# Where the weights, the normed input and the arena begin in a partition: 0 and 32 bytes past a multiple of 64, in a 1-core fp32 kernel of five network layers

## What is computed

```python
for i in range(DEPTH):                       # 4 layers
    h = _rmsnorm(x, norm_mix_g[i])
    mix = ...                                # h @ w_in, the mixer itself, @ w_out
    x = x + mix
    x = x + _sqrelu_mlp(_rmsnorm(x, norm_mlp_g[i]), mlp_w1[i], mlp_w2[i])

def _sqrelu_mlp(h, w1, w2):
    return jnp.square(jax.nn.relu(h @ w1)) @ w2
```

## The kernel before

| Tensors | Role in line 432 | Before | mod 64 | After | mod 64 |
|---|---|---|---|---|---|
| raw / wh / wl | weights (stationary) | 16544 / 32928 / 49312 | 32 | 16512 / 32896 / 49280 | 0 |
| x / xh / xl | moving (xh, xl) | 65696 / 82080 / 98464 | 32 | the same | 32 |
| rs, acc, tmp, hf, ones and other small ones | - | 114848 and on | 32 | the same | 32 |
| arena: hh, hl, yh, yl, mh, ml, the mixers' tensors | moving | 131200 and on | 0 | 131232 and on | 32 |

## Time and profile before

### The profile page before, as it was taken

The page is one execution under the profiler, slowest core; times in us unless marked ns, Lnnn a source line. Parts: engine busy times, 40 slices in busy tenths (PEclk is TensorE's granted clock), DMA queues, the critical chain, the costliest instruction groups (busy, mean ns, idle before and its releaser), DMA issues.

```text
span 4019.4 us, 50973 instructions
## 1 busy us (share of the span) xinstructions
PE 3751.5 (93%) x20972; PEld 3021.8 (75%) x20972; DVE 1907.7 (47%) x2121; ACT 1127.8 (28%) x1283; POOL 438.5 (11%) x425
## 2 busy tenths in 40 slices
PE   7999999899999999998999997867899988989998
PEld 5678888688888888866788785645699956768886
DVE  7654333353445534366534345566343356455342
ACT  2632223131222322235322222233211122333221
POOL 1111111020110201110101110000001000102011
PEclk9999999699999999999999997988999989999999
DMA  3132323032322333221333220211300013323221
GB/s 126 55 96 94 94 94 100 32 94 94 94 94 95 95 102 95 96 86 55 108 99 94 84 84 0 89 55 58 110 2 3 3 36 136 103 80 100 94 94 63
DMA packets 295680, 320.51 MB, mean 80 GB/s; under 512 B 5811, under 2 KB 287798, under 8 KB 295255
## 3 DMA queue, kind: packets, MB, share of 16 engines
q1 hardware_dynamic: 288439, 295.92, 23.3%
q0 software_dynamic: 3616, 15.86, 1.2%
q10 hardware_dynamic: 3456, 6.29, 0.4%
HBM read 307.57 MB, written 10.49 MB: 79 GB/s over the span
## 4 chain that ended last, share of the span: by engine, by line
PE 87%; DVE 7%; ACT 4%; issue 1%; DMA 0%; SPq 0%; POOL 0%; ACTq 0%; DVEq 0%; POOLq 0%
PE ps L432 70%; PE ps L773 2%; PE ps L1392 1%; PE ps L419 1%; PE ps L1411 1%; DVE wl L386 1%; PE ps L1364 1%; PE ps L1410 1%; PE ps L1371 1%; PE ps L1053 1%; ACT wh L382 1%; PE ps L1032 1%; PE ps L891 1%; PE ps L892 1%; DVE rs L456 0%
## 5 line engine op out<-in xcount | busy, mean ns | idle before, releaser
L432 PE MATMUL ps<-xh,wh 128*128 128x512 f32 x2424 | 970.1, 400 | 66.8 <-DVE wl L386 52.0
L432 PE MATMUL ps<-xl,wh 128*128 128x512 f32 x2424 | 956.4, 395 | 0.0
L432 PE MATMUL ps<-xh,wl 128*128 128x512 f32 x2424 | 954.4, 394 | 0.0
L386 DVE TENSOR_TENSOR wl<-raw,wh 128x2048 fp32r<-128x2048 f32 x283 | 657.0, 2322 | 457.9 <-ACT wh L382 457.2
L382 ACT ACTIVATE wh<-raw 128x2048 fp32r<-128x2048 f32 x283 | 539.6, 1909 | 883.2 <-PE ps L432 756.2
L432 PEld LDWEIGHTS ps<-xh,wh 128*128 128x128 f32 x2424 | 464.0, 191 | 181.1 <-issue 73.2
L432 PEld LDWEIGHTS ps<-xl,wh 128*128 128x128 f32 x2424 | 463.3, 191 | 102.8 <-issue 6.8
L432 PEld LDWEIGHTS ps<-xh,wl 128*128 128x128 f32 x2424 | 462.8, 191 | 98.3
L432 PE MATMUL ps<-hh,wh 128*128 128x512 f32 x1280 | 506.3, 396 | 0.0
L432 PE MATMUL ps<-hl,wh 128*128 128x512 f32 x1280 | 506.2, 396 | 0.0
L432 PE MATMUL ps<-hh,wl 128*128 128x512 f32 x1280 | 506.2, 396 | 0.0
(11 more groups left out here) (352 smaller groups left out, 3973.7 us busy)
## 6 DMA issues: line engine op xcount, KB each, us to landing
raw<-in_mlp_w SPq DMA_DIRECT2D x128, 1024.0 KB, 5.6
raw<-in_ffn_w SPq DMA_DIRECT2D x32, 1024.0 KB, 5.3
raw<-in_w_in SPq DMA_DIRECT2D x31, 1024.0 KB, 5.3
raw<-in_a_w_in SPq DMA_DIRECT2D x20, 1024.0 KB, 5.1
raw<-in_c_w_in SPq DMA_DIRECT2D x12, 1024.0 KB, 5.2
raw<-in_a_w_out SPq DMA_DIRECT2D x16, 640.0 KB, 4.6
raw<-in_b_w_in SPq DMA_DIRECT2D x8, 1024.0 KB, 5.2
raw<-in_xa_wkv SPq DMA_DIRECT2D x8, 1024.0 KB, 5.3
```

The source lines that it names most:

```text
L386: nc.vector.tensor_tensor(wl[:, p.slot(su)], raw[:, p.slot(su)], wh[:, p.slot(su)], ALU.subtract).then_inc(lower, 1)
L432: last = nc.tensor.matmul(banks[mt][:, 0:st.n], wt[:, slot, k, mt * P:mt * P + P], ops[oi][:, kk, 0:st.n], start=k == 0 and su == 0 and n_ ...
```

## The change

Three addresses are set in another way; no instruction, loop, wait or size is touched, and the instructions stand in the same order on every engine. The first tensor begins at the next multiple of 64 instead of 32 bytes past one. 32 bytes are left free between `wl` and `x`, so that `x` and all that follows stay where they were. The arena begins 32 bytes past the next multiple of 64.

```diff
@@ -91,7 +91,9 @@
 def build(nc, a, out):
     ctx = ExitStack()
     base = nc.sbuf_base
-    PERS = (base + 63) // 32 * 32
+    LINE = 64
+    HALF = LINE // 2
+    PERS = (base + LINE - 1) // LINE * LINE
     used = [PERS]
@@ -111,6 +113,7 @@
     WH_AT = used[0]
     wh = pers("wh", [P, 2, 8, 256], F32R)
     wl = pers("wl", [P, 2, 8, 256], F32R)
+    used[0] += HALF
     x = pers("x", [P, ND, T])
     XH_AT = used[0]
     xh = pers("xh", [P, ND, T], F32R)
@@ -127,7 +130,7 @@
     prm = [pers(f"prm{i}", [P, P]) for i in range(4)]
     small = pers("small", [P, 64])
     c8 = pers("c8", [P, 2, 2 * NR])
-    ARENA = used[0]
+    ARENA = (used[0] + LINE - 1) // LINE * LINE + HALF
     LIMIT = nc.sbuf_top
```

## The result

The changed kernel takes 4055.87 us (median of 5 runs) against 4022.86 us before (5 runs): a ratio of 1.0085 with a 95% interval of 1.0073 to 1.0098, which is 33 us slower (29 to 39). I had forecast 75 us faster.

A forecast was written before the change was run, and what follows sets the result against it. The prediction took TensorE, 87% of the span, as the bound. Its terms, -24.2 (x), -53.3 (h and y), +3.5 (waits and clock) and -0.5 (256-column stages), gave -74.5 us: 3948 us, range 3905 to 4030.

The forecast's parts named there:

- Weights to 0, under x: x matmuls, 512 columns: moving the weights' start to 0 shortens each from 226.7 to 223.3 ns, -24.2 us.
- A block touches 9 pieces of 64 bytes or 8: Weight reads: 512 bytes touch 9 pieces from start 32, 8 from start 0; one piece less saves 8 clocks.
- Arena to 32 with weights at 0: h and y matmuls: they get the same pair of starts as x, so 223.3 ns each, -53.3 us.
- the slower rival: x stages: unlike starts of weights and moving operand slow x to 233.3 ns, h and y stay; 4070 us, chance 0.20.
- the two streams must stand alike: x stages: unlike starts of weights and moving operand cost x +48.5 us, h and y stay; 4070 us, chance 0.20.
- only the moving start matters: 512-column matmuls: h and y come down to x's 226.7 ns, x stays; 3988 us, chance 0.22.
- No change: 512-column matmuls: addresses don't matter, x and h differ for another reason; 4023 us, chance 0.06.
- A larger gain: 512-column matmuls: weights at 0 remove half of x's surplus, 220.0 ns; 119 us less, 3905 us, chance 0.08.
- the split: Splitting of weights on ScalarE and VectorE: covered by TensorE's work, taken 0, bounds -0.8 and +0.8 us.
- the fetches: Fetches into `raw`, now beginning on 64: landing in 5.6 us, cost 0 while under some 6 us of slack.
- The two memory stages: 256-column memory stages: they exchange their pairs of starts, 192 x 1.7 us each way, net nothing.
- The swapped x stage: 256-column x stage with operands swapped: pair goes from (32, 32) to stationary 32, moving 0; -0.5 us.

The follow-up runs named there:

- e4: Against the kernel before: weights at 0, x at 64 and arena at 96 modulo 128; 4033.48 us (one run).
- e9: Against the kernel before: weights at 0, xh and xl at 192, arena at 160 modulo 256; 4059.05 us (one run).
- e3: Against the kernel before: weights, x and arena all begin at a multiple of 64; 3985.1 us, ratio 0.9912.
- e1: Against the kernel before: the arena alone begins 32 bytes later; 3986.61 us, ratio 0.9915.
- e2: Against the kernel before: the weights alone begin at a multiple of 64; 4030.42 us, ratio 1.0024.
- e7: Against the kernel before: 32 bytes left free ahead of `xl`, which also moved the arena by 32 bytes; 4027.17 us (one run).
- e8: Against the kernel before: arena 32 bytes later, and one term of three uses 64 of the 128 stationary columns; 4020.62 us (one run).
- e10: Against the kernel before: all starts alike, and all three terms of h use 64 of the 128 stationary columns; 3996.53 us (one run).

## Why the prediction was wrong, point by point

- **The step that failed is "Weights to 0, under x".** I took 223.3 ns for the pair (0, 32) at 512 columns, by carrying over the 3.3 ns between two rows at 256 columns. It measured 233.3 ns: +49 us in place of -24. The transfer itself was wrong. At 256 columns both unlike pairs that I had are shorter than the like one (120.0 ns at distance 0; 116.7 and 118.4 in the earlier trace rows), and at 512 columns every unlike pair measured is longer. The later runs bear the reversal out in most cases (in e4, 113.3 ns with weights moving at a distance of 192), but not in all: in e9, with weights moving at a distance of 96, 144 matmuls take 17.28 us, 120.0 ns, like the like pair. Nor does the distance modulo 256 settle the step at 256 columns: 32 took 116.7 ns before and after, and 117.8 in e4. I had both orders before me: the earlier trace rows said that unlike is slow at 512 columns, that it is fast at 256. That reversal should have told me that the 256-column rows can't price the other shape. The rows of e9, at 120.0 ns:

```profile
3561.12 0.28 PE L420 MATMUL ps<-wh,mh 128*128 128x256 f32 x1
...
3578.40 0.28 PE L420 MATMUL ps<-wh,mh 128*128 128x256 f32 x1
```

- **"A block touches 9 pieces of 64 bytes or 8"** has no support. e3, with 8 pieces, and e1, with 9, have the same step.
- **"Arena to 32 with weights at 0"** was sized at -53 us and is 0: h and y only went from one unlike distance, 224, to another, 32. The mechanism that I had put down as the slower rival priced this right.
- **The rival "the two streams must stand alike"** gave 233.3 ns for x, h and y, and units of 11.20 us; this is what the profile shows, and e1, e2 and e3 tell it from every other reading that I had. I had given it 0.20. Its price of 4070 us was 14 too high: of its +48.5 us on x the count above has 45.5 (49.0 less the 3.5 of matmuls that only changed their clock), and the other matmuls and x at the half clock go against it. What I missed in it is the period, 256 bytes and not 64; at a distance of 64 bytes the step is 228.9 ns.
- **The rival "only the moving start matters"** falls with e2: h is fast with its moving start at 0. **"No change"** falls with e1. **"A larger gain"** has nothing for it: no 512-column stage in any run went below 226.7 ns.
- **The Trainium skill** (SBUF — State Buffer, "Who interferes with whom") has the two reads of PE on independent ports. The step here goes by how the two starts stand to each other, 226.7 to 237.3 ns by address alone, so the two reads are not independent in time for fp32r at 512 columns; that PE waits for no other engine is not put in doubt by these runs. The Trainium skill (TensorE: Matmul & The Clock Gate, "Wait — 56ns, not 53.3ns?") gives 215.7 ns at 512 columns, and names neither an address nor fp32r. No 512-column stage here came down to it.
- **Small readings.** In 2580 to 2850 us there are 643 x matmuls in the trace, not 12 units or 576; at 3.33 ns that is 2.1 us in place of 1.9. The 3.5 us between span and runs mix two things: in the changed kernel's profiled run the time is 1.7 us above the span, and the rest is how one run differs from another. Neither moves the forecast by more than 2 us.
- **Right:** that the path is TensorE's and that a step per matmul is what moves the time; that nothing but addresses sets the 6.7 ns; that the split (VectorE 2323 ns, before 2322), the fetches (5.6 us) and the waits for `wl` (66.9 us) would not move. The two memory stages did exchange their steps: with mh moving, 144 matmuls now take 16.79 us, 116.6 ns. The swapped x stage went from 120.0 to 118.3 ns, as taken.

```profile
3532.53 0.28 PE L435 MATMUL ps<-mh,wh 128*128 128x256 f32 x1
...
3549.32 0.28 PE L435 MATMUL ps<-mh,wh 128*128 128x256 f32 x1
```

**What stays open.** Why like starts give the shortest steady pattern at 512 columns, and what sets the step at 256. e7, e8 and e10 show that it is a pattern of moving reads and weight loads together and not a sum of prices; what within TensorE or SBUF they meet at was not looked at further. Whether `raw` must share the start was not tried apart from the rest; nothing in ScalarE's or VectorE's durations points to it.

## What to carry to other kernels

Where TensorE streams fp32r matmuls of 512 columns back to back, put the stationary and the moving tensors at the same address modulo 256, and every slice of them at a multiple of that (in this kernel all slices lie at multiples of 512; no run tried others). Here e1's one line gave 2.9% on each h and y matmul and 0.9% on the kernel. Read the step from start to start over a whole unit, stage by stage, and put the addresses beside it; the busy time of a matmul group hides it. And take a price only from rows of the same shape: the same distance, 32 bytes, was faster than the like start at 256 columns and slower at 512.

## What the runs showed that I had not expected

- The like start matters modulo 256 bytes: distance 0 or 256 gives 226.7 ns, 128 some 232.5, 64 gives 228.9.
- 4 bytes off is the worst distance measured: 237.3 ns.
- One term of three with an unlike start takes all three from 226.7 to some 233 ns.
- Halving the weight load makes a 512-column matmul slower: 230.0 ns against 226.7.
- At 256 columns it is mostly the other way: 120.0 ns with like starts, down to 113.3 ns with unlike ones, and 120.0 again at a distance of 96.
